# One subtraction of the expert stage moved ahead of its neighbour in VectorE's program (MLA, gMLP and hierarchical MoE block, Trainium2)

## The chip, the cores and the metric

The kernel runs on one core of one Trainium2 chip. The metric is device time in microseconds. One core has five engines that run programs of their own and meet at semaphores: TensorE (PE in the rows; its weight loads are PEld), VectorE (DVE), ScalarE (ACT), GpSimd (POOL) and SyncE (SP, here only the issuer of DMAs). 16 DMA engines move the data.

## What is computed

The reference is one layer of a hybrid encoder on 1024 tokens of width 1024, float32, followed by a final RMSNorm. A combined projection feeds latent attention (8 heads) and a spatial gating unit; both are gated, projected and added to the input. Then comes the part that matters here, a mixture of experts: each token goes to 2 of 8 experts of the best of 4 groups (32 experts, each with 1024x256 gate and up weights and a 256x1024 down weight).

```python
def expert_block(args):
    xb, e = args
    hid = jax.nn.silu(xb @ w_eg[e]) * (xb @ w_eu[e])
    return hid @ w_ed[e]
...
ys = lax.map(expert_block, (xs, blk_e)).reshape(p_rows, d)
out = jnp.zeros((n, d), h.dtype).at[buf_tok].add(ys * buf_w[:, None])
```

## The kernel before

Products of float32 are made of three matmuls of float32r operands (`mm3`, lines 367 to 371): each operand is split into a high part (a copy that rounds) and a low part (the operand minus the high part), and high x high, high x low and low x high are added up. ScalarE writes the high parts and VectorE the low ones in the expert stage.

The stages run one after the other: norm, projections, attention, gating unit, mixing, output projection with the router, ranking of the tokens, experts (stage "E"), and the combine stage (stage "C"), which gathers two expert results per token, adds them and normalizes.

The expert stage works on blocks of 128 gathered rows, one expert each: the 32 experts and the overflow blocks. In the profiled execution there are 36 blocks. `experts(eng, body)` (lines 388 to 399) is the same loop for each engine: four blocks written out, a loop over groups of four, four blocks written out again for the end. `left(n)` says whether there is a block n further on. In each block j the engines do the following, each in its own fixed order:

- SyncE (lines 496 to 513) loads the up weight of block j+2, the down weight of j+1 and the gate weight of j+3, 1024 KB each, into six buffers `raw_e`. A load waits until VectorE has made the low part of the piece that had the buffer (`w_lo_ready`).
- TensorE (lines 852 to 901): `columns(0, j+1)` (gate), `hidden_in(j)` (two transposes of the hidden rows into `ps` bank 4), `columns(1, j+1)` (up), `down(j)` (12 matmuls with the hidden rows and the down weight), `rows_in(j+3)` (eight transposes of the gathered rows into banks 0 and 1). `columns` waits for `xst_ready` and `w_lo_ready`; `down` waits for `hidt_ready`; `rows_in(j+3)` waits until `rows_low(j+2)` has read the banks.
- ScalarE (lines 1091 to 1126): `hidden_high(j)`, the high part of the up weight of j+2, `silu(j+1)`, the high part of the down weight of j+1, `rows_out(j)` (the result of block j, `y<-ps` in the rows), the high part of the gate weight of j+3, `rows_high(j+3)`.
- VectorE (lines 1550 to 1580): `hidden_low(j)` (L1568, `hidt_lo`), `rows_low(j+2)` (L1558, `xst_lo`), `low(1, j+2)`, `hidden(j+1)` (L1564), `low(2, j+1)`, `low(0, j+3)` (L1554, `we_lo`; 0, 1 and 2 are gate, up and down).
- GpSimd (lines 1671 to 1695) gathers the rows of block j+4 and scatters the result of block j, both by indirect DMA.

`rows_low(j)` subtracts the high part of the rows, as ScalarE wrote it, from the transposed rows in PSUM; it waits for `xst_hi_ready`, which `rows_high(j)` raises. `hidden_low(j)` waits for `hidt_hi_ready`, which `hidden_high(j)` raises.

Of the kernel before, what the change touches and what calls it, by code (L numbers as in the profile page):

```python
# [93 lines left out]
def build(nc, a, out, stop_after=None):  # L94
    base = 16512

    with ExitStack() as ctx:
# [5 lines left out]
        def sem(name):  # L103
            if name not in sems:
                sems[name] = ctx.enter_context(nc.semaphore(name))
            return sems[name]
# [268 lines left out]
        def piece(g, it, j, last=False):  # L375


            if isinstance(it, int) and it == 0 and j == 0 and g < 2:
                return g, g
            c = 3 * j + (-1, 0, 4)[g] - 2 * last  # L380
            return c, it * 12 + c

        def wait(eng, name, value):

            if not (isinstance(value, int) and value <= 0):
                eng.wait_ge(sem(name), value)

        def experts(eng, body):

            for j in range(4):  # L390
                body(0, j, lambda n: True)
            eng.wait_ge(sem("tab_read"), 1)
            end = eng.value_load(n_last[0:1, 0:1], min_val=NE // 4 - 1, max_val=NBLK // 4 - 1)
            with eng.Fori(1, end) as it:
                for j in range(4):
                    body(it, j, lambda n: True)
            for j in range(4):
                body(end, j, lambda n, j=j: j + n < 4)
            return end
# [755 lines left out]
        def _(dve):  # L1155
# [393 lines left out]
            if "E" in on:  # L1549
                def low(g, it, j, last=False):  # L1550

                    c, n = piece(g, it, j, last)
                    dve.wait_ge(sem("w_hi_ready"), n + 1)
                    dve.tensor_tensor(we_lo[c % 4][:, :], raw_e[c % 6][:, :], we_hi[c % 4][:, :].bitcast(F32), ALU.subtract).then_inc(sem("w_lo_ready"), 1)  # L1554

                def rows_low(it, j):
                    dve.wait_ge(sem("xst_hi_ready"), it * 4 + (j + 1))
                    dve.tensor_tensor(xst_lo[j % 2][:, :, :], ps[:, 0:2, :].rearrange("p b (k c) -> p (b k) c", c=P),  # L1558
                                      xst_hi[j % 2][:, :, :].bitcast(F32), ALU.subtract).then_inc(sem("xst_ready"), 1)

                def hidden(it, j):
                    dve.wait_ge(sem("sg_ready"), it * 4 + (j + 1))
                    wait(dve, "hid_tr", it * 4 + j)
                    dve.tensor_tensor(hid[:, :], ps[:, 2 + j % 2, DE:2 * DE], sg[:, :], ALU.mult).then_inc(sem("hid_ready"), 1)  # L1564

                def hidden_low(it, j):
                    dve.wait_ge(sem("hidt_hi_ready"), it * 4 + (j + 1))
                    dve.tensor_tensor(hidt_lo[:, :, :].rearrange("p a b -> p (a b)"), ps[:, 4, 0:2 * P],  # L1568
                                      hidt_hi[:, :, :].rearrange("p a b -> p (a b)").bitcast(F32), ALU.subtract).then_inc(sem("hidt_ready"), 1)

                def expert(it, j, left):
                    hidden_low(it, j)
                    if left(2):
                        rows_low(it, j + 2)
                        low(1, it, j + 2)
                    if left(1):
                        hidden(it, j + 1)
                        low(2, it, j + 1, not left(2))
                    if left(3):
                        low(0, it, j + 3)  # L1580

                low(0, 0, 0)
                low(1, 0, 0)
                rows_low(0, 0)
                rows_low(0, 1)
                low(0, 0, 1)
                low(1, 0, 1)
                hidden(0, 0)
                low(2, 0, 0)
                low(0, 0, 2)  # L1590
                experts(dve, expert)
            if "C" in on:
                dve.wait_ge(sem("g_full"), 32)
# [142 lines left out]
```

## Time and profile before

| | |
|---|---|
| time, median of 3 runs | 1241.35 us (1240.95 to 1247.44) |
| the profiled execution | 1241.35 us, its span 1239.2 us |
| granted TensorE clock, mean over the span | 0.948 |
| busy: TensorE, VectorE, ScalarE, GpSimd | 89%, 58%, 46%, 28% of the span |
| expert stage | about 835 to 1191 us of the span |

The span runs from the first to the last instruction; the time of the execution is a little longer. Busy shares of the whole span mix stages with different limits, so the stage around the change is read by itself. A row of the timeline has the start in us from the span's start, the duration in us, engine, line, operation, output and inputs; in brackets stands the idle time before it and who ended that.

### The profile page before, as it was taken

The numbers are of one execution on the slowest core, as the hardware profiler recorded it, in microseconds if no ns is written. First come the engines' busy times: TensorE is split into PE (matmuls) and PEld (weight loads), VectorE is DVE, ScalarE is ACT, GpSimd is POOL, SyncE is SP. The second block draws the span as 40 slices with busy tenths as digits, with TensorE's granted clock in tenths as the row PEclk, the third lists the DMA queues.
The fourth block names the chain that finished last, engine by engine and source line by source line (L and its number), as shares of the span: only waits on it lengthen the run. The fifth ranks groups of instructions, "written<-read, shape, count | busy, mean of one in ns | idle before, by whom it ended". The sixth has DMA issues, their size and how long they took to land.

```text
span 1239.2 us, 18129 instructions
## 1 busy us (share of the span) xinstructions
PE 1098.4 (89%) x6835; PEld 958.9 (77%) x6835; DVE 713.9 (58%) x832; ACT 565.3 (46%) x756; POOL 345.6 (28%) x276
## 2 busy tenths in 40 slices
PE   3998999999998899999998999419999999999930
PEld 3876888888877788888887888419999999889930
DVE  6875666666055721111114223468888888888938
ACT  5235556655044200000003222307888888778823
POOL 3103222113232223332230000122444444555410
PEclk7998999999999999999999999659999999999975
DMA  8010000021104111111112412447999999999747
GB/s 246 2 28 11 7 7 7 7 69 35 51 1 112 35 34 49 37 50 51 51 50 91 120 69 82 165 169 269 398 387 370 357 354 368 347 366 364 301 151 282
DMA packets 93131, 184.27 MB, mean 149 GB/s; under 512 B 29712, under 2 KB 67088, under 8 KB 79248
## 3 DMA queue, kind: packets, MB, share of 16 engines
q1 hardware_dynamic: 82704, 166.65, 38.6%
q0 software_dynamic: 10368, 16.80, 3.7%
q8 instruction: 41, 0.67, 0.2%
q14 instruction: 18, 0.15, 0.0%
HBM read 177.12 MB, written 27.26 MB: 165 GB/s over the span
## 4 chain that ended last, share of the span: by engine, by line
PE 72%; DVE 12%; DMA 7%; ACT 4%; issue 3%; SPq 1%; POOL 1%; ACTq 0%; POOLq 0%; DVEq 0%
PE ps L369 21%; PE ps L371 21%; PE ps L370 21%; DMA raw_e<-in_w_exp_gate_dram 5%; PE ps L858 2%; PE ps L658 2%; DVE pt_lo L1319 1%; PE ps L818 1%; DVE negm L1274 1%; DVE we_lo L1554 1%; ACT we_hi L1096 1%; SPq L348 1%; ACT prob L987 1%; DVE q_tmp L1265 1%; DVE acc L1599 1%
## 5 line engine op out<-in xcount | busy, mean ns | idle before, releaser
L1554 DVE TENSOR_TENSOR we_lo<-raw_e,we_hi 128x2048 fp32r<-128x2048 f32 x108 | 246.9, 2289 | 41.6 <-ACT we_hi L1096 41.2
L1096 ACT ACTIVATE we_hi<-raw_e 128x2048 fp32r<-128x2048 f32 x108 | 206.4, 1911 | 27.3 <-DMA raw_e<-in_w_exp_gate_dram 11.4
L369 PE MATMUL ps<-ht_hi,w_hi 128*128 128x512 f32 x448 | 176.2, 393 | 0.4 <-DVE ht_lo L1192 0.4
L371 PE MATMUL ps<-ht_hi,w_lo 128*128 128x512 f32 x448 | 174.5, 389 | 0.0
L370 PE MATMUL ps<-ht_lo,w_hi 128*128 128x512 f32 x448 | 174.4, 389 | 0.0
L369 PE MATMUL ps<-we_hi,xst_hi 128*128 128x256 f32 x576 | 168.9, 293 | 0.0
L370 PE MATMUL ps<-we_lo,xst_hi 128*128 128x256 f32 x576 | 163.0, 283 | 0.0
L371 PE MATMUL ps<-we_hi,xst_lo 128*128 128x256 f32 x576 | 162.9, 283 | 0.0
L363 POOL CAST w_hi<-raw 128x1024 fp32r<-128x1024 f32 x36 | 40.5, 1125 | 302.5 <-PE ps L371 269.8
L369 PEld LDWEIGHTS ps<-we_hi,xst_hi 128*128 128x128 f32 x576 | 110.8, 192 | 0.0
L370 PEld LDWEIGHTS ps<-we_lo,xst_hi 128*128 128x128 f32 x576 | 110.6, 192 | 0.0
L371 PEld LDWEIGHTS ps<-we_hi,xst_lo 128*128 128x128 f32 x576 | 110.3, 192 | 0.0
L1398 DVE TENSOR_TENSOR mix<-ps,mix 128x512 f32<-128x512 f32 x16 | 11.1, 691 | 168.1 <-PE ps L371 168.1
L369 PEld LDWEIGHTS ps<-ht_hi,w_hi 128*128 128x128 f32 x448 | 84.3, 188 | 18.1 <-issue 1.0
L371 PEld LDWEIGHTS ps<-ht_hi,w_lo 128*128 128x128 f32 x448 | 84.1, 188 | 17.7
L370 PEld LDWEIGHTS ps<-ht_lo,w_hi 128*128 128x128 f32 x448 | 84.3, 188 | 17.1 <-issue 0.2
L364 POOL TENSOR_TENSOR w_lo<-raw,w_hi 128x1024 fp32r<-128x1024 f32 x36 | 87.4, 2428 | 2.9
L1053 ACT ACTIVATE mix<-ps 128x512 f32<-128x512 f32 x16 | 8.7, 597 | 146.9 <-PE ps L371 146.9
L1684 POOL COPY ycol<-yidx 128x1 uint32 (+1 forms) x36 | 28.3, 786 | 150.3 <-ACT y L1114 150.3
L1319 DVE TENSOR_TENSOR pt_lo<-ps,pt_hi 128x512 fp32r<-128x512 f32 (+2 forms) x96 | 50.4, 553 | 20.3 <-ACT pt_hi L1013 20.0
L369 PE MATMUL ps<-we_hi,hidt_hi 128*128 128x512 f32 x144 | 57.1, 397 | 5.4 <-DVE hidt_lo L1568 5.2
L1673 POOL COPY xcol<-xidx 128x1 uint32 (+1 forms) x36 | 50.7, 1409 | 36.1 <-DVE xidx L1548 34.6
(284 smaller groups left out, 2511.6 us busy)
## 6 DMA issues: line engine op xcount, KB each, us to landing
raw_e<-in_w_exp_gate_dram SPq DMA_DIRECT2D x36, 1024.0 KB
raw_e<-in_w_exp_up_dram SPq DMA_DIRECT2D x36, 1024.0 KB
raw_e<-in_w_exp_down_dram SPq DMA_DIRECT2D x36, 1024.0 KB
raw<-in_w_in_dram SPq DMA_DIRECT2D x27, 512.0 KB, 3.8
yin<-y_dram SPq DMA_DIRECT2D x16, 512.0 KB, 6.6
xin<-in_x_dram SPq DMA_DIRECT2D x8, 512.0 KB, 6.8
raw<-in_w_out_dram SPq DMA_DIRECT2D x8, 512.0 KB, 3.8
xre<-in_x_dram SPq DMA_DIRECT2D x8, 512.0 KB, 4.2
```

What stands on the lines that cost most here:

```text
L363: pool_link(pool, pool.tensor_copy(w_hi[n % 3][:, :, :], raw[n % 3][:, :, :]))
L364: pool.tensor_tensor(w_lo[n % 3][:, :, :], raw[n % 3][:, :, :], w_hi[n % 3][:, :, :].bitcast(F32), ALU.subtract).then_inc(sem("w_split"), 1)
L369: pe.matmul(dst, st[0], mv[0], start=first, stop=False)
L370: pe.matmul(dst, st[0], mv[1], start=False, stop=False)
L371: return pe.matmul(dst, st[1], mv[0], start=False, stop=last)
L658: mm = pe.transpose(ps[:, bank_of(0, c0 + c), (j % 4) * P:(j % 4) * P + P], prob[s % 2][:, j * P:(j + 1) * P], ident[:, :])
L858: mm = pe.transpose(ps[:, k // 4, (k % 4) * P:(k % 4) * P + P], v[:, k, :], ident[:, :])
L1096: act.activation(we_hi[c % 4][:, :], raw_e[c % 6][:, :], ACT.Copy).then_inc(sem("w_hi_ready"), 1)
L1319: dve.tensor_tensor(pt_lo[cc % 4][:, 0:w, :].rearrange("p a b -> p (a b)"), ps[:, bank_of(0, cc), 0:w * P], pt_hi[cc % 4][:, 0:w, :].rearr ...
L1554: dve.tensor_tensor(we_lo[c % 4][:, :], raw_e[c % 6][:, :], we_hi[c % 4][:, :].bitcast(F32), ALU.subtract).then_inc(sem("w_lo_ready"), 1)
L1673: pool.tensor_copy(xcol[j % 4][:, :], xidx[:, column(it, j)]).then_inc(sem("xcol_ready"), 1)
L1684: pool.tensor_copy(ycol[j % 2][:, :], yidx[:, column(it, j)]).then_inc(sem("ycol_ready"), 1)
```

## The change

In VectorE's program of the expert stage, `rows_low` of block j+3 is issued at the end of the body of block j, after `low(0, it, j + 3)`, instead of `rows_low` of block j+2 after `hidden_low` of block j. Since bodies follow each other, the same call moves from behind `hidden_low(j+1)` in the next body to a place ahead of it. `rows_low(0, 2)`, which had its place in the first body, is now issued ahead of the loop.

```diff
                 def expert(it, j, left):
                     hidden_low(it, j)
                     if left(2):
-                        rows_low(it, j + 2)
                         low(1, it, j + 2)
                     if left(1):
                         hidden(it, j + 1)
                         low(2, it, j + 1, not left(2))
                     if left(3):
                         low(0, it, j + 3)
+                        rows_low(it, j + 3)
...
                 hidden(0, 0)
                 low(2, 0, 0)
                 low(0, 0, 2)
+                rows_low(0, 2)
                 experts(dve, expert)
```

## Rows read from the trace of the kernel before

**Rows 1.** the page, its first line
```profile
span 1239.2 us, 18129 instructions
```

**Rows 2.** stretches of two experts each: busy us of each engine, granted clock, DMA
```profile
core 0: us, PE busy (x) PEld busy (x) DVE busy (x) ACT busy (x) POOL busy (x), PEclk, DMA share, GB/s
...
876.71:895.96 19.25, 19.25 (x143) 18.26 (x142) 17.05 (x12) 16.16 (x15) 8.43 (x9) 1.00 1.02 402
1011.41:1030.71 19.30, 19.30 (x142) 18.31 (x142) 17.03 (x13) 16.30 (x16) 8.51 (x9) 1.00 0.97 362
1050.64:1071.26 20.62, 20.01 (x146) 18.83 (x146) 17.26 (x12) 16.23 (x15) 10.43 (x9) 1.00 0.99 351
1071.26:1091.97 20.71, 19.74 (x143) 18.38 (x142) 17.27 (x13) 16.23 (x15) 10.36 (x9) 1.00 0.97 347
```

**Rows 3.** VectorE in order of time, steady part: start, us, engine, line, operation
```profile
934.52 2.30 DVE L1554 TENSOR_TENSOR we_lo<-raw_e,we_hi 128x2048 fp32r<-128x2048 f32 x1 [1.18 <-ACT we_hi L1096]
936.75 0.41 DVE L1568 TENSOR_TENSOR hidt_lo<-ps,hidt_hi 128x256 fp32r<-128x256 f32 x1
937.08 1.21 DVE L1558 TENSOR_TENSOR xst_lo<-ps,xst_hi 128x1024 fp32r<-128x1024 f32 x1
938.21 2.28 DVE L1554 TENSOR_TENSOR we_lo<-raw_e,we_hi 128x2048 fp32r<-128x2048 f32 x1
...
944.06 2.29 DVE L1554 TENSOR_TENSOR we_lo<-raw_e,we_hi 128x2048 fp32r<-128x2048 f32 x1 [1.04 <-ACT we_hi L1096]
946.27 0.42 DVE L1568 TENSOR_TENSOR hidt_lo<-ps,hidt_hi 128x256 fp32r<-128x256 f32 x1
```

**Rows 4.** ScalarE in order of time, the same part
```profile
941.20 1.03 ACT L1114 ACTIVATE y<-ps 128x1024 f32<-128x1024 f32 x1 [0.57 <-PE ps L371]
942.12 1.91 ACT L1096 ACTIVATE we_hi<-raw_e 128x2048 fp32r<-128x2048 f32 x1
943.92 1.02 ACT L1100 ACTIVATE xst_hi<-ps 128x1024 fp32r<-128x1024 f32 x1
945.18 0.39 ACT L1109 ACTIVATE hidt_hi<-ps 128x256 fp32r<-128x256 f32 x1 [0.25 <-PE ps L878]
```

**Rows 5.** TensorE in order of time: first matmul of down of experts 0, 9, 29
```profile
851.66 0.40 PE L369 MATMUL ps<-we_hi,hidt_hi 128*128 128x512 f32 x1
...
938.24 0.40 PE L369 MATMUL ps<-we_hi,hidt_hi 128*128 128x512 f32 x1
...
1135.71 0.47 PE L369 MATMUL ps<-we_hi,hidt_hi 128*128 128x512 f32 x1
```

**Rows 6.** who waited for whom: TensorE from 1030 to 1140, VectorE from 840 to 1200
```profile
PE ps L369 <- DVE hidt_lo L1568: 3.1, 6, 0.8
...
DVE hidt_lo L1568 <- ACT hidt_hi L1109: 1.7, 1, 1.7
```

**Rows 7.** ScalarE in order of time, at results 0 and 33 and in between
```profile
854.62 1.03 ACT L1114 ACTIVATE y<-ps 128x1024 f32<-128x1024 f32 x1 [0.49 <-PE ps L371]
...
1048.70 1.91 ACT L1096 ACTIVATE we_hi<-raw_e 128x2048 fp32r<-128x2048 f32 x1 [0.57 <-DMA raw_e<-in_w_exp_gate_dram]
...
1138.73 1.03 ACT L1114 ACTIVATE y<-ps 128x1024 f32<-128x1024 f32 x1 [0.36 <-PE ps L371]
...
1177.21 1.03 ACT L1114 ACTIVATE y<-ps 128x1024 f32<-128x1024 f32 x1 [0.56 <-PE ps L371]
```

**Rows 8.** VectorE in order of time, at expert 0 and around the late part
```profile
850.52 0.42 DVE L1568 TENSOR_TENSOR hidt_lo<-ps,hidt_hi 128x256 fp32r<-128x256 f32 x1
...
1040.25 2.29 DVE L1554 TENSOR_TENSOR we_lo<-raw_e,we_hi 128x2048 fp32r<-128x2048 f32 x1 [1.03 <-ACT we_hi L1096]
...
1132.84 2.29 DVE L1554 TENSOR_TENSOR we_lo<-raw_e,we_hi 128x2048 fp32r<-128x2048 f32 x1 [1.37 <-ACT we_hi L1096]
...
1135.05 0.42 DVE L1568 TENSOR_TENSOR hidt_lo<-ps,hidt_hi 128x256 fp32r<-128x256 f32 x1
```

**Rows 9.** SyncE's queue in order of time: one load of a gate weight
```profile
1033.19 0.34 SPq L504 DMA_DIRECT2D raw_e<-in_w_exp_gate_dram  x1
```

## The prediction

> **What bounds the kernel now.** I read the page first for where the span goes; it is 1239.2 us long [rows 1]. The change touches only VectorE's program in the expert stage, from about 835 us to 1191 us of the span, so I then cut that stage into stretches [rows 2]. In the nine from 857 to 1031 us, two of them shown, TensorE is busy from end to end at a granted clock of 1.00. `down` of expert 0 starts at 851.66 and `down` of expert 9 at 938.24 [rows 5]: 86.58 us for nine, 9.62 us each, and that is TensorE's own work. After 1050 us two experts take 20.62 and 20.71 us, and TensorE idles for 0.61 and 0.97 us of them. The 16 DMA engines are 0.97 to 1.02 busy in the rows of both regimes.
>
> Next the order of time. In the first regime ScalarE's high part of a gate weight starts without waiting for its load, and VectorE idles 1.04 to 1.18 us before its low part, until ScalarE has made the high part [rows 3, 4]. In the second, ScalarE waits for the load itself (0.57 us at 1048.70) and TensorE waits for `hidt_lo` six times, 3.1 us together [rows 6, 7]. What this second regime costs shows in ScalarE's copies of the expert results: result 0 starts at 854.62 and result 33 at 1177.21 [rows 7]. That is 322.59 us for 33 experts; at 9.62 us they would take 317.46 us. So late loads cost 5.1 us now.
>
> **What the change does, as rows.** It removes and adds no instruction: 36 times `rows_low` before and after, on VectorE alone, each 1.21 us long and 1.13 us from its start to that of the next (937.08 to 938.21) [rows 3]. No DMA is issued by VectorE, so no queue has more or fewer transfers. Only the order differs.
>
> Now, VectorE runs: low part of gate weight j+3, `hidden_low(j+1)`, `rows_low(j+3)`, low part of up weight j+3. At 934.52 the gate part starts, at 936.75 `hidden_low`, at 937.08 `rows_low`, at 938.21 the up part [rows 3]. In the new program `rows_low(j+3)` stands between the gate part and `hidden_low(j+1)`. The pair of neighbours is swapped, nothing else.
>
> Does the swap use idle time? The idle 1.04 to 1.18 us lies before the gate part, which is ahead of both, so it doesn't. A gap between the gate part and `hidden_low` would be filled, but there is none: ScalarE's high half of the hidden rows is done at 945.57 (945.18 plus 0.39), before `hidden_low` gets its turn at 946.27 [rows 3, 4]. In the whole stage VectorE waits for that half just once, 1.7 us, in the tail, where no `rows_low` is left to fill it [rows 6]. And the new wait of `rows_low` is met: the high half of the rows of expert j+3 ends at 944.94 (943.92 plus 1.02), 1.3 us before the slot at 946.27 [rows 4]. So the up part starts when it did, the buffers of the loads come free when they did relative to the gate part, and VectorE gains nothing.
>
> What it loses: `hidden_low` starts 1.13 us later, and behind it TensorE waits with the whole of `down` and what follows it in order (the transposes for the next rows, the next gate columns). In the steady regime the margin is this: `hidden_low` starts at 936.75 and takes 0.41, so it ends at 937.16; `down` starts at 938.24 [rows 3, 5]. An end on VectorE is followed by TensorE's start 0.24 us later: 1135.05 plus 0.42 is 1135.47, and TensorE starts at 1135.71 [rows 5, 8]. The margin is 938.24 - 937.16 - 0.24 = 0.84 us, and the swap takes 1.13 us. It no longer fits, by 0.29 us in this expert and by 0.2 us in the next.
>
> A stall of TensorE doesn't just add up, because what feeds `hidden_low` hangs on the previous `down` too: end of `down` -> ScalarE's result copy -> ScalarE's high gate part -> VectorE's low gate part -> `hidden_low` -> next `down`. So I take the loop:
> - start of `down` to start of the result copy, after a stall: 1135.71 to 1138.73 = 3.02 us [rows 5, 7]; without one 938.24 to 941.20 = 2.96 us [rows 4, 5]
> - result copy to start of the high gate part: 941.20 to 942.12 = 0.92 us; from there to the low part: 944.06 - 942.12 = 1.94 us; from there to VectorE's next slot: 946.27 - 944.06 = 2.21 us [rows 3, 4]
> - new: `rows_low` in that slot 1.13 us; `hidden_low` 0.42 us; to TensorE 0.24 us
>
> Sum: 3.02 + 0.92 + 1.94 + 2.21 + 1.13 + 0.42 + 0.24 = 9.88 us per expert. Without the 1.13 it is 8.75, under TensorE's 9.62, and it is hidden now. With it, the loop is the bound: 0.26 us per expert more than TensorE's own work. Whether one takes 2.96 or 3.02 for `down`, the loop is 9.82 to 9.88 us; I take 3.02, since TensorE will have stalled each time.
>
> The first expert: VectorE's `hidden_low(0)` starts at 850.52, and `down(0)` at 851.66 [rows 5, 8]. After the swap: 850.52 + 1.13 + 0.42 + 0.24 = 852.31, so `down(0)` is 0.65 us later.
>
> The late loads. In the new program experts come every 9.88 us from the first on. By result 20 the loads are then asked for 0.65 + 20 x 0.26 = 5.9 us later than now, and the DMA engines, busy all the time, have worked off as much of what stands in their queue. From 1040.25 to 1132.84 loads let an expert through every 10.29 us (nine experts) [rows 8]; against 9.88 they fall behind by 0.41 x 9 = 3.7 us, less than the 5.9 us in hand. So the 5.1 us that late loads cost now is not paid again: it is already waited out. This is where I choose; the other end is the first rival below.
>
> That the queue is long enough for this, rows show: a gate load issued at 1033.19 is waited for until 1048.70, 15.5 us for one megabyte, while the stage moves 347 to 402 GB/s, so some five loads stand in line (15.5 us at 350 GB/s are 5.4 MB) [rows 2, 7, 9]. The Trainium skill, "DMA: Bandwidth & Descriptors" (Bandwidth), gives a single load of 1 MB 6.15 us (issued from GpSimd); if a load took that here, no queue would stand, nothing would be stored up, and the sum would be the first rival's. The 15.5 us speak against it.
>
> **Sum.** New result 33: 854.62 + 0.65 + 0.06 (copy after a stalled `down`) + 33 x 9.88 = 1181.37 us, against 1177.21: 4.2 us later. Behind it come two experts without `rows_low` ahead of their `hidden_low`, the same as now, and the unchanged combine stage. The profiled execution took 1241.35 us with a span of 1239.2; it is also the median of the three runs shown. So 1241.35 + 4.2 = 1245.5 us. With 9.82 us per expert it is 2.2 us instead, so the forecast's own range is 1243.5 to 1247.
>
> **Rivals.**
> - *Late loads add to the loop* (chance 0.17). If the pace of the loads from 1040 us on is a fixed time from issue to landing and not a queue, nothing is in hand. Then results 0 to 20 come at 9.88 us (855.3 + 20 x 9.88 = 1052.9), nine at 10.29 (1145.5), four at 9.88 (1185.0): 7.8 us later, 1249.2 us. For it: issue to landing stays near 15 us. Against: that is also what five loads in line give.
> - *The DMA engines hide it* (chance 0.10). If the transfers as a whole set the pace all through the stage, 0.26 us per expert costs nothing: 1241.4 us. It decides at 9.88 us per expert for the bytes that an expert needs. For it: DMA 0.97 to 1.02 busy. Against: TensorE has no gap up to 1031 us, and 402 GB/s were moved in one of those stretches [rows 2]. The Trainium skill, same page (Where 436 GB/s comes from), puts about 358 GB/s as HBM's share of one core; by that the loads would bind from the first expert. The 402 GB/s here don't bear it out.
> - *Faster* (chance 0.05). If `hidden_low` now waits for ScalarE after the gate part, `rows_low` fills that wait; the up part, and with it a load, then comes up to 1.13 us earlier. It decides where the high half of the hidden rows ends after the gate part; now it ends 0.7 us before it (945.57 against 946.27) [rows 3, 4]. At best it gives back all 5.1 us of late loads: 1236.2 us.
>
> The forecast itself has 0.64. The last 0.04 is a stall that costs more than these rows say.
>
> **How the numbers follow.** A run of this kernel can be told from no change at about 0.5%, 6.2 us. The forecast is inside that, but for 0.04 at its upper edge. Slower: 0.17 + 0.04 + 0.04 = 0.25. Faster: 0.05. Same: 0.60 + 0.10 = 0.70. The range from 1241 to 1250 us takes in the forecast, the late loads and the hidden case, and leaves out the faster one and the worst.
>
> **What would show it.** In the new trace: `xst_lo` before `hidt_lo` in each expert, with no idle between; TensorE waiting for `hidt_lo` some 0.2 to 0.3 us in nearly every expert from the first; `down` to `down` 9.88 us from 860 us on; ScalarE's idle time before `we_hi` for loads nearly gone; the up parts next to the gate parts as now. The prediction is wrong if the experts still come every 9.62 us up to 1031 us, or if they come every 10.3 us after 1050 us.

## The result and the profile after

The changed kernel takes 1251.49 us, median of 19 runs (1247.43 to 1255.94); the kernel before takes 1244.79 us, median of 19 (1240.17 to 1248.97). The ratio is 1.0055, 95% interval 1.0041 to 1.0068: slower by 6.8 us, 5.1 to 8.5 us. The forecast was 4.2 us slower, 1245.5 us, range 1241 to 1250, so the sign and the mechanism held, and the size and the range did not.

The profiled execution has a span of 1248.4 us. In VectorE's order of time, two looped experts (start, us, engine, line; to be held against [rows 3]):

```profile
940.97 2.29 DVE L1554 TENSOR_TENSOR we_lo<-raw_e,we_hi 128x2048 fp32r<-128x2048 f32 x1 [1.47 <-ACT we_hi L1096]
943.17 1.22 DVE L1558 TENSOR_TENSOR xst_lo<-ps,xst_hi 128x1024 fp32r<-128x1024 f32 x1
944.31 0.42 DVE L1568 TENSOR_TENSOR hidt_lo<-ps,hidt_hi 128x256 fp32r<-128x256 f32 x1
944.64 2.28 DVE L1554 TENSOR_TENSOR we_lo<-raw_e,we_hi 128x2048 fp32r<-128x2048 f32 x1
...
950.88 2.29 DVE L1554 TENSOR_TENSOR we_lo<-raw_e,we_hi 128x2048 fp32r<-128x2048 f32 x1 [1.42 <-ACT we_hi L1096]
953.09 1.22 DVE L1558 TENSOR_TENSOR xst_lo<-ps,xst_hi 128x1024 fp32r<-128x1024 f32 x1
954.22 0.41 DVE L1568 TENSOR_TENSOR hidt_lo<-ps,hidt_hi 128x256 fp32r<-128x256 f32 x1
```

`xst_lo` and `hidt_lo` have changed places, back to back. The idle time ahead of the gate part hasn't been used; it has grown from 1.04 to 1.18 us to 1.42 to 1.47 us, because ScalarE's gate part comes later.

TensorE around the starts of `down` in the same two experts (against [rows 5]):

```profile
944.57 0.28 PE L371 MATMUL ps<-we_hi,xst_lo 128*128 128x256 f32 x1
944.97 0.47 PE L369 MATMUL ps<-we_hi,hidt_hi 128*128 128x512 f32 x1
...
954.57 0.28 PE L371 MATMUL ps<-we_hi,xst_lo 128*128 128x256 f32 x1
954.88 0.47 PE L369 MATMUL ps<-we_hi,hidt_hi 128*128 128x512 f32 x1
```

Matmuls of the column phase start 0.12 us apart, but 0.40 and 0.31 us pass between its last one and the first of `down`: TensorE stalls for 0.28 and 0.19 us. The first of `down` takes 0.47 us, where it took 0.40 before [rows 5]. `hidden_low` ends at 944.73 and 954.63, so TensorE starts 0.24 and 0.25 us after it.

ScalarE's result copies (against [rows 4, 7]):

```profile
938.11 1.03 ACT L1114 ACTIVATE y<-ps 128x1024 f32<-128x1024 f32 x1 [0.94 <-PE ps L371]
939.03 1.90 ACT L1096 ACTIVATE we_hi<-raw_e 128x2048 fp32r<-128x2048 f32 x1
...
948.02 1.03 ACT L1114 ACTIVATE y<-ps 128x1024 f32<-128x1024 f32 x1 [0.94 <-PE ps L371]
```

From `down` (944.97) to the copy (948.02) 3.05 us pass, in the next expert 3.13 us. The whole trace has this pair in turn: 9.91 and 9.99 us per looped expert. And ScalarE waits for nothing but TensorE now (waits from 860 to 1195 us, in us, times, longest):

```profile
ACT y L1114 <- PE ps L371: 31.3, 34, 1.1
ACT sg L1105 <- PE ps L371: 25.0, 34, 2.5
ACT hidt_hi L1109 <- PE ps L878: 9.0, 34, 2.1
```

No wait for a load is left. The stretches of two experts (columns as in [rows 2]) say the same:

```profile
1017.71:1037.61 19.90, 19.75 (x142) 18.36 (x142) 17.01 (x13) 16.24 (x15) 8.42 (x8) 1.00 0.95 353
1057.51:1077.40 19.89, 19.74 (x142) 18.36 (x142) 17.00 (x13) 16.24 (x14) 8.42 (x8) 1.00 0.99 365
1077.40:1097.31 19.91, 19.76 (x142) 18.38 (x142) 17.02 (x13) 16.25 (x15) 8.42 (x8) 1.00 0.96 359
```

One even pace of 19.9 us stands where there were two (19.24 and 20.7 us), at the same granted clock of 1.00. The last number of each row below is the median time of the loads from issue to landing, here of those issued between 1050 and 1140 us:

```profile
raw_e<-in_w_exp_gate_dram SPq DMA_DIRECT2D x9, 1024.0 KB, 9.9
raw_e<-in_w_exp_up_dram SPq DMA_DIRECT2D x9, 1024.0 KB, 9.8
raw_e<-in_w_exp_down_dram SPq DMA_DIRECT2D x9, 1024.0 KB, 10.9
```

Over the whole stage the medians are 8.6, 7.9 and 8.7 us. So loads do slow down in the late part of the changed kernel too, but none is waited for. In the kernel before, the gate load issued at 1033.19 was waited for until 1048.70, 15.5 us later [rows 7, 9].

**Where the time went, as the traces have it.** I take the span apart at ScalarE's copies of results 0 and 33 (two executions of each kernel, both traced):

| us | before | before, again | changed | changed, again |
|---|---|---|---|---|
| result 0 starts | 854.62 | 858.03 | 859.04 | 858.89 |
| result 0 to result 33 | 322.59 | 321.34 | 327.75 | 327.46 |
| span | 1239.2 | 1242.9 | 1248.4 | 1249.5 |

Result 0 to result 33 is the part that the change acts on: 5.2 us more in the first traces of the two kernels and 6.1 us more in the second ones. At expert 0 some 0.6 us come on top: the last column matmul starts at 855.38, `down` would follow at 855.50 and follows at 855.97, and its copy comes 0.11 us late. Together that is 5.7 and 6.7 us, and 6.8 (5.1 to 8.5) were measured. The rest of the span's difference in the first pair of traces lies ahead of the changed instructions. The two traces of before differ between results 0 and 33 as well, since late loads cost 5.1 us in the one and 3.9 us in the other (against 33 x 9.62 us).

### The profile page after: what moved, and what is told of

Its sections match the earlier page's. It is cut to its first block, busy times and chain, and to the rows that moved or that the text cites. A ratio compares the mean times of both kernels' runs of the same rounds, so it can differ in the third digit from the quotient of the medians.

```text
span 1248.4 us, 18136 instructions
## 1 busy us (share of the span) xinstructions
PE 1108.9 (89%) x6835; PEld 963.9 (77%) x6835; DVE 712.3 (57%) x832; ACT 564.8 (45%) x756; POOL 327.0 (26%) x276
## 4 chain that ended last, share of the span: by engine, by line
PE 78%; DVE 11%; ACT 4%; issue 2%; DMA 2%; SPq 1%; POOL 0%; ACTq 0%; POOLq 0%; DVEq 0%
PE ps L369 24%; PE ps L371 23%; PE ps L370 23%; PE ps L858 3%; PE ps L658 2%; DVE pt_lo L1319 1%; PE ps L818 1%; DVE negm L1274 1%; SPq L348 1%; DVE q_tmp L1265 1%; ACT prob L987 1%; DVE acc L1600 1%; DVE res L1610 1%; DVE acc L1601 1%; PE ps L667 1%
## 5 line engine op out<-in xcount | busy, mean ns | idle before, releaser
L1674 POOL COPY xcol<-xidx 128x1 uint32 (+1 forms) x36 | 61.5, 1709 | 36.6 <-DVE xidx L1548 34.6
L1013 ACT ACTIVATE pt_hi<-ps 128x512 fp32r<-128x512 f32 (+2 forms) x96 | 43.5, 488 | 36.8 <-PE ps L658 36.8
```

The lines of the kernel that those rows point to most:

```text
L1013: act.activation(pt_hi[cc % 4][:, 0:w, :].rearrange("p a b -> p (a b)"), ps[:, bank_of(0, cc), 0:w * P], ACT.Copy).then_inc(sem("pt_hi_rea ...
L1674: pool.tensor_copy(xcol[j % 4][:, :], xidx[:, column(it, j)]).then_inc(sem("xcol_ready"), 1)
```

## The experiments

Each ratio is to the kernel before on the same chip, with its 95% interval.

**1. The changed kernel again.** No edit.

> The changed kernel once more, unaltered. Theory A (the loop from down through the result copy, the gate parts, rows_low and hidden_low to the next down sets the pace): result 0 to result 33 takes 327 to 328 us again, 9.9 to 10.0 us per expert once the looped code runs, and the time is 1.004 to 1.007 of before. Theory B (part of what was measured is how the expert stage was entered, 3.9 us later in the first profile with the same instructions up to there): the entry differs from one execution to the next, and result 0 to result 33 does not.

Ratio 1.0042 (1.0018 to 1.0066). Result 0 to 33 took 327.46 us against 327.75. The entry was 858.89 us. The kernel before once more, for its profile:

> The kernel before once more, unaltered, for its profile. Theory B: the entry of the expert stage (result 0) lies some us elsewhere than the 854.62 us of the first profile, and result 0 to result 33 takes 322 to 324 us, by how late the loads come.

Its time was 1245.06 us, result 0 at 858.03, result 0 to 33 in 321.34 us; that is 0.7 us under the range that was given for it. So the first trace of before, from which the prediction started, entered the stage 3.4 us earlier than another execution of the same instructions: 3.4 us that no term of the sum could hold.

The two traces of before show where these 3.4 us come from (columns as in [rows 2]; each pair has the first trace, then the second):

```profile
676.00:683.00 7.00, 5.70 (x25) 4.74 (x26) 5.85 (x7) 4.12 (x5) 0.00 (x0) 1.00 0.54 153
676.00:683.00 7.00, 5.86 (x14) 4.64 (x15) 5.63 (x6) 3.89 (x4) 0.00 (x0) 0.52 0.57 155
...
839.60:843.20 3.60, 3.60 (x32) 3.60 (x32) 3.37 (x3) 1.26 (x2) 0.00 (x0) 1.00 0.00 0
839.60:843.20 3.60, 3.16 (x15) 3.19 (x16) 0.42 (x2) 1.02 (x1) 0.00 (x0) 0.50 0.17 43
```

In the second trace TensorE's granted clock fell to 1.2 GHz (0.50) at about 676 us for some 7 us, where the first kept 2.4 GHz (1.00): twelve matmuls started 0.43 us apart instead of 0.23, which is some 2.4 us. TensorE had been idle for 3.2 us before them in both traces. Ahead of the expert stage both ran at 0.50, and the clock was back at 1.00 at 839.6 us in the first trace and at 843.2 us in the second, where the same matmuls then came another 0.8 us later. That is 3.2 of the 3.4 us. The same happened behind the changed part: in the second trace the clock fell at 1191.4 us, in the middle of the last `down`, and its result copy started 4.60 us after the start of `down` instead of 3.04 us. So the spans differ by 3.7 us: 3.4 ahead, 1.3 less between results 0 and 33, 1.6 behind. Why the clock fell in one execution and not in the other is not known. The traces of the changed kernel were not taken apart in this way.

**2. Half of `rows_low` ahead, half behind.** `rows_part(j, b)` subtracts in the columns of bank b; `rows_first(it, j)` waits for `xst_hi_ready` and does those of bank 0. `rows_first(0, 2)` is issued ahead of the loop.

```diff
-                        rows_low(it, j + 2)
+                        rows_part(j + 2, 1)
                         low(1, it, j + 2)
...
                         low(0, it, j + 3)
+                        rows_first(it, j + 3)
```

> rows_low in two halves of 128x512: one ahead of hidden_low, one behind it. Theory A: a half takes 0.60 us of VectorE's time ahead of hidden_low (between the 0.34 of 256 columns and the 1.13 of 1024), less than the margin of 0.84 us, so experts come every 9.62 us up to about 1040 us and the time is that of before, 0 to 1 us more (ratio 1.000 to 1.001). Rival C (each bit put ahead of hidden_low costs in proportion): half the loss, 3 to 4 us (ratio 1.003).

```profile
930.92 0.68 DVE L1562 TENSOR_TENSOR xst_lo<-ps,xst_hi 128x512 fp32r<-128x512 f32 x1
931.52 0.41 DVE L1578 TENSOR_TENSOR hidt_lo<-ps,hidt_hi 128x256 fp32r<-128x256 f32 x1
931.85 0.68 DVE L1562 TENSOR_TENSOR xst_lo<-ps,xst_hi 128x512 fp32r<-128x512 f32 x1
```

That is VectorE in one expert: the half takes 0.60 us from its start to the next. TensorE in the same expert:

```profile
932.40 0.28 PE L371 MATMUL ps<-we_hi,xst_lo 128*128 128x256 f32 x1
932.52 0.40 PE L369 MATMUL ps<-we_hi,hidt_hi 128*128 128x512 f32 x1
```

`down` follows its predecessor in 0.12 us: no stall. `hidden_low` ended at 931.93, 0.59 us ahead (0.45 us in every second expert), of which TensorE needs 0.24. Results came every 9.62 us on average up to about 1070 us, and result 0 to 33 took 323.03 us, 0.4 us more than in the first trace of before and 1.7 us more than in the second. In the trace the margin is a threshold, not a proportion. The ratio, 1.0022 (1.0003 to 1.0041), doesn't say so by itself: it lies above the 1.000 to 1.001 of theory A, and its interval takes in that and the 1.003 of rival C. What the case costs while loads are late, from 1070 us on, was not taken apart.

**3. The loads made light.** All weight loads but the first six move half of their columns; half of the weight data is left out.

```diff
-                    sp.dma_start(raw_e[c % 6][:, :], w_d[...])
+                    cols = 2048 if isinstance(n, int) and n < 6 else 1024
+                    sp.dma_start(raw_e[c % 6][:, 0:cols], w_d[...][:, 0:cols])
```

> The kernel before, with all weight loads but the first six cut to half their columns; it leaves out half of the weight data, and its output is another. Theory A: the late loads go, experts come every 9.62 us to the end, result 0 to result 33 takes 317.5 us, and the time is 5.1 us less than before (ratio 0.996). Rival D (what slows the experts after 1040 us is not the loads): no difference.

> The changed kernel, with the same loads cut to half their columns. Theory A (its loads are never late, what they lost is already waited out): same pace as the changed kernel, 9.95 us per expert, the time 1.004 to 1.007 of before, and some 11 us more than the light form of the kernel before (33 experts by 0.33 us, and 0.6 us at the first). Rival E (transfers still set a part of the changed kernel's pace): 2 to 5 us less than the changed kernel.

Before with light loads: ratio 0.9959 (0.9942 to 0.9976), 5.1 us less; result 0 (860.82) to result 33 (1178.27) takes 317.45 us, the 33 x 9.62 of the prediction. The changed kernel with light loads: 1.0049 (1.0031 to 1.0066); 857.23 to 1184.44 is 327.21 us, the pace of the changed kernel. The late loads cost the kernel before some 5 us (3.0 to 7.2 by the interval, 5.1 and 3.9 by the two traces) and the changed one nothing that can be measured (1.0049 against 1.0042 on the same chip). Freed of them the two kernels stand 9.8 us apart in this part; in the full kernels 5.2 and 6.1 us.

**4. One more subtraction, ahead or behind.** `rows_twice` makes the subtraction first into a spare tile, then as usual. In the changed kernel (ahead); in the kernel before (behind) the call for j+2 is replaced in the same way.

```diff
-                        rows_low(it, j + 3)
+                        rows_twice(it, j + 3)
```

> The changed kernel with the subtraction of rows_low made twice ahead of hidden_low, the first time into a spare tile. Theory A (a closed loop through hidden_low): each expert takes the whole 1.13 us more, 10.9 us in the first three and 11.08 us in the looped code, so 33 x 1.13 + 1.13 = 38 us more than the changed kernel, ratio to before 1.034 to 1.038. Rival F (a part of what stands ahead of hidden_low is made up for somewhere else): clearly less than 1.13 us per expert.

> The kernel before with the same second subtraction, but behind hidden_low, where rows_low stands. Theory A (place, not work): VectorE's 1.04 to 1.18 us of idle time per expert takes it up, the gate part starts 0 to 0.1 us later, less than the margin of 0.84 us; experts come every 9.62 to 9.65 us up to about 1040 us, 0 to 2 us more in all, ratio 1.000 to 1.002. Rival G (VectorE's total work is what costs): tens of us, as in the kernel with the subtraction ahead.

Ahead: ratio 1.0387 (1.0351 to 1.0423). Experts come every 10.87 us in the code written out and every 11.06 us in the loop; against 9.76 and 9.95 us that is 1.11 us each. I had given 1.034 to 1.038: between results 0 and 33 the trace has 36.7 us more than the changed kernel's first, as forecast, and the rest of the excess lies outside this part, in a median of four runs. VectorE in one of them:

```profile
934.11 1.22 DVE L1565 TENSOR_TENSOR spare<-ps,xst_hi 128x1024 fp32r<-128x1024 f32 x1
935.24 1.22 DVE L1558 TENSOR_TENSOR xst_lo<-ps,xst_hi 128x1024 fp32r<-128x1024 f32 x1
936.37 0.41 DVE L1576 TENSOR_TENSOR hidt_lo<-ps,hidt_hi 128x256 fp32r<-128x256 f32 x1
```

Behind: ratio 1.0011 (0.9991 to 1.0031).

```profile
939.47 0.42 DVE L1576 TENSOR_TENSOR hidt_lo<-ps,hidt_hi 128x256 fp32r<-128x256 f32 x1
939.80 1.22 DVE L1565 TENSOR_TENSOR spare<-ps,xst_hi 128x1024 fp32r<-128x1024 f32 x1
940.94 1.22 DVE L1558 TENSOR_TENSOR xst_lo<-ps,xst_hi 128x1024 fp32r<-128x1024 f32 x1
```

The same 36 added instructions cost some 41 us in one place (1293.01 against the changed kernel's 1251.49 us) and nothing that can be measured in the other. What costs is the place, not VectorE's work.

**5. The result copy taken out of the loop.** ScalarE makes the high gate part of expert j+3 ahead of the result copy of expert j.

```diff
-                    rows_out(it, j, not left(1))
                     if left(3):
                         high(0, it, j + 3)
+                    rows_out(it, j, not left(1))
+                    if left(3):
                         rows_high(it, j + 3)
```

> The changed kernel with ScalarE's high gate part of expert j+3 ahead of its result copy of expert j, so that the copy's 0.92 us is no longer in the loop. Theory A: the loop falls from 9.95 to 9.03 us, under TensorE's 9.62, experts come every 9.62 us and the loads are late again from about 1040 us on: ratio to before 0.999 to 1.001. Rival H (the copy isn't in the loop, what costs is only hidden_low's own delay): as the changed kernel, 1.005.

> The kernel before with the same order on ScalarE. Theory A: the margin of hidden_low grows from 0.84 to 1.8 us, which changes nothing up to 1040 us; while loads are late it lets VectorE be 0.9 us later before TensorE waits, so 0 to 1 us less, ratio 0.999 to 1.000. Rival H: no difference.

On the changed kernel: ratio 1.0011 (0.9993 to 1.0028). The loss is gone, with `rows_low` still ahead of `hidden_low`. ScalarE:

```profile
928.50 1.92 ACT L1096 ACTIVATE we_hi<-raw_e 128x2048 fp32r<-128x2048 f32 x1 [0.56 <-PE ps L371]
930.32 1.01 ACT L1114 ACTIVATE y<-ps 128x1024 f32<-128x1024 f32 x1
```

and VectorE:

```profile
930.45 2.29 DVE L1555 TENSOR_TENSOR we_lo<-raw_e,we_hi 128x2048 fp32r<-128x2048 f32 x1 [0.19 <-ACT we_hi L1096]
932.66 1.22 DVE L1559 TENSOR_TENSOR xst_lo<-ps,xst_hi 128x1024 fp32r<-128x1024 f32 x1
933.79 0.41 DVE L1569 TENSOR_TENSOR hidt_lo<-ps,hidt_hi 128x256 fp32r<-128x256 f32 x1
```

`hidden_low` now ends at 934.20 and `down` starts at 935.17, so 0.97 us pass instead of 0.24. Experts come every 9.62 us until the loads are late, from 1060 us on. This refutes the rival that the copy isn't in the loop. On the kernel before: 1.0010 (0.9988 to 1.0032), no gain. I had given 0.999 to 1.000. Its trace has one expert of 11.56 us at the start; TensorE waits there for gathered rows, whose gather stands behind the scatter of the later copy in GpSimd's program. That this ate the gain is argued from the trace, not tried; a gain of 0 to 1 us would not show in this interval anyway.

**6. `rows_low` moved the other way, behind the low part of the up weight.**

```diff
-                        rows_low(it, j + 2)
                         low(1, it, j + 2)
+                        rows_low(it, j + 2)
```

> The kernel before with rows_low moved the other way, behind the low part of the up weight. Theory A: hidden_low is not delayed, so nothing is lost: 9.62 us per expert up to 1040 us, ratio 0.999 to 1.001. The low up part comes at most 0.45 us earlier, since ScalarE's high up part ends only then, and its load with it, while the next down load goes 0.7 us later. Rival K (moving rows_low at all costs): 1.003 or more.

A miss: ratio 1.0071 (1.0046 to 1.0096). Experts take 10.03 us on average, and result 0 to result 33 takes 331.03 us, some 3 us more than with the change itself; in the times the intervals of the two overlap. TensorE at the end of `down`:

```profile
932.66 0.39 PE L371 MATMUL ps<-we_hi,hidt_lo 128*128 128x512 f32 x1
933.17 1.05 PE L858 MATMUL ps<-ident,xs 128*128 128x128 f32 x7
```

and who its weight loads waited for from 860 to 1200 us:

```profile
PEld ps L858 <- DVE xst_lo L1558: 15.7, 29, 0.6
```

`rows_in(j+3)` may write banks 0 and 1 of `ps` only when `rows_low(j+2)` has read them. In this order it ends at 933.11 (931.89 plus 1.22), about when TensorE wants the banks. `rows_low` has a deadline of its own, and I had looked only at that of `hidden_low`. This is read from the trace; no further run tested it.

**7. Eight experts written out.** The changed kernel with `body(0, j)` and `body(1, j)` written out ahead of the loop, which then starts one group later. Executed once.

```diff
-            for j in range(4):
-                body(0, j, lambda n: True)
+            for i in range(2):
+                for j in range(4):
+                    body(i, j, lambda n: True)
```

> The changed kernel with eight experts written out ahead of the loop instead of four. In the changed kernel TensorE starts 0.05 us after the end of hidden_low in the experts written out (0 to 3, 9.76 us each) and 0.24 us after it in the looped ones (9.95 us on average). Theory I (it is the code: constant wait values against ones from a register): experts 4 to 7 now also have 0.05 us and 9.76 us. Rival J (it is the position in the stage, such as the state of the transfers): they keep 0.24 us.

Experts 4 to 7 take 9.77, 9.74, 9.74 and 9.74 us now, and those after them 9.87 to 9.99 us. VectorE and TensorE in expert 6:

```profile
913.76 0.41 DVE L1569 TENSOR_TENSOR hidt_lo<-ps,hidt_hi 128x256 fp32r<-128x256 f32 x1
```

```profile
914.10 0.28 PE L371 MATMUL ps<-we_hi,xst_lo 128*128 128x256 f32 x1
914.23 0.50 PE L369 MATMUL ps<-we_hi,hidt_hi 128*128 128x512 f32 x1
```

`hidden_low` ends at 914.17 and TensorE starts 0.06 us later. It is the code and not the position: the same experts in the looped form start 0.24 to 0.25 us after the end. In the code written out the start of `down` stands just 0.13 us behind the matmul before it, so the stall hardly shows there; it shows in the first matmul of `down`, which takes 0.50 us and is followed by the next at 914.56, 0.33 us later, where 0.23 us pass without a stall. Which of the loop's instructions takes the 0.19 us was not tried.

## Why the prediction was wrong in size and right in kind

- *A swap of two neighbours, no idle time used.* Right: the rows after show it, and the idle time before the gate part grew.
- *A margin of 0.84 us, and 1.13 us put into it.* Right. The half that fits the margin brings no stall in the first regime (experiment 2), and once the margin is used up a further 1.13 us costs 1.11 us in each expert (4).
- *The loop from `down` over result copy, gate parts, `rows_low` and `hidden_low` to the next `down` becomes the bound.* Right, shown by taking one link out (5) and by lengthening another (4).
- *9.88 us per expert.* This step of the sum failed. The term from the start of `down` to the result copy was set at 3.02 us from a single stalled expert; in the loop it is 3.05 and 3.13 us in turn, 3.09 us on average. The other terms came as given: 0.92 from copy to high gate part, 1.94 to the low part, 2.21 to the slot, 1.13, 0.42 and 0.24. The loop is 9.95 us. For the 30 looped experts that is 2.1 us more. The first three, in code written out, took 9.76 us, 0.4 us less together, since TensorE started 0.05 us after `hidden_low` there; that the two errors partly cancel is luck. The prediction has 3.45 us for this part (33 x 9.88 - 322.59), and 3.45 + 2.1 - 0.4 = 5.2 us, which is what the first two traces show between results 0 and 33. The trace of before already had the alternation. Both readings of the prediction, 2.96 and 3.02 us, are of experts with an odd number (9 and 29); in expert 10, without a stall, 3.03 us pass:

```profile
947.86 0.40 PE L369 MATMUL ps<-we_hi,hidt_hi 128*128 128x512 f32 x1
...
950.89 1.03 ACT L1114 ACTIVATE y<-ps 128x1024 f32<-128x1024 f32 x1 [0.64 <-PE ps L371]
```

- *0.65 us at the first expert.* 0.47 us of stall, and 0.11 us on the copy: 0.58 us where 0.65 + 0.06 was forecast. The 0.24 us to TensorE's start were 0.05 us in this expert too.
- *The 5.1 us of late loads are not paid again.* Right, the choice that mattered most: light loads take some 5 us off the kernel before and nothing measurable off the changed one (3). The first rival, a fixed time from issue to landing, is refuted: it gave 10.29 us per expert after 1050 us, and they took 9.95; the loads issued then landed in 9.8 to 10.9 us (medians) instead of some 15. The second rival, transfers that hide it, falls too: the change cost 6.8 us, and half the weight data did not change the pace of the changed kernel. The faster case had no wait to fill.
- *1241.35 us as the base.* This term failed by the most: it is 3.4 us under the median of the 19 runs. Of the 6.0 us between 1245.5 and 1251.49 us, 3.4 come from there and 2.6 from the effect: 4.2 us forecast, 6.8 us measured (5.1 to 8.5). Of these 2.6 us the pace of the experts explains 1.7 (2.1 - 0.4); the rest is not more than the late loads of the kernel before vary from one execution to the next (5.1 and 3.9 us) and lies within the interval. The range took in the unknown costs, but not how far one execution lies from the median, and its upper end was 1.5 us too low. The three runs of before spread over 6.5 us, which was warning enough. Part of that spread is TensorE's granted clock outside the changed part, as the two traces of before show (experiment 1).
- *The bound of 0.5%.* The case "same" had the highest chance, 0.70, and rested on 4.2 us against 6.2. The measured 0.55% lies just past that bound, its interval on both sides of it.

No version here beats both kernels: the later copy brings the changed order back to the time of before (1.0011, 0.9993 to 1.0028), no further. The light forms leave work out and aren't versions.

## What to carry to other kernels

An instruction moved within an in-order engine has two prices to look up: what waits behind its new place, and what waits for itself. Compare each with the slack of that consumer: below it the move is free, above it the rest is paid once per turn, and if the producer's inputs hang on the consumer's last turn, write down that loop and sum it. A cost that comes from a queue being behind isn't added to a slower pace, it is replaced by it. For a forecast in microseconds, take the base and its spread from all runs, not from the one that was traced.

## What the runs showed of the hardware that I had not expected

- TensorE's first matmul after a wait for VectorE started 0.05 to 0.06 us after the producer's end in code written out, and 0.24 to 0.25 us after it in the looped code (experiment 7 moves four experts from the one to the other).
- Two executions of the kernel before put result 0 at 854.62 and 858.03 us, with the same instructions up to there. In the second the granted clock was 0.52 from 676 to 683 us, where it was 1.00 in the first, and it came back from 0.50 to 1.00 at 843.2 instead of 839.6 us. At 0.50 matmuls of 512 columns started 0.43 us apart, at 1.00 0.23 us.
- A stall of TensorE once per expert, 0.2 to 0.3 us in the changed kernel and 1.3 to 1.4 us with the subtraction made twice, left the granted clock at 1.00 in the whole expert part.
- Half of a 128x1024 subtraction from PSUM took VectorE 0.60 us from start to start, the whole 1.13 us.
